# Sharing the experts' weight split between VectorE and GpSimd: 1280 and 768 of 2048 columns

## The reference

```python
def moe_ffn(x, router_w, w1, w2):
    xt = x.reshape(-1, d)
    logits = (xt @ router_w).astype(jnp.float32)
    top_logit, top_idx = lax.top_k(logits, TOP_K)
    gates = jax.nn.softmax(top_logit, axis=-1)
    ...
    def expert_group(args):
        x_blk, e = args
        return swiglu(x_blk, w1[e], w2[e])
    yb = lax.map(expert_group, (xb, blk_expert)).reshape(cap, d)
    ...

for layer in range(DEPTH):
    h = h + parallel_mixer(h, ...)
    h = h + memory_cross_attention(h, mem, ...)
    hn = rms_norm(h, ffn_norm_w[layer])
    if layer % 2 == 0:
        h = h + swiglu(hn, ffn_w1[layer // 2], ffn_w2[layer // 2])
    else:
        h = h + moe_ffn(hn, moe_router[layer // 2], moe_w1[layer // 2], moe_w2[layer // 2])
return rms_norm(h, final_norm_w)
```

## Time and profile before

| | us |
|---|---|
| median of three runs | 1603.72 |
| lowest, highest run | 1603.5, 1607.22 |
| the profiled execution | 1604.92 |
| its span, first to last instruction | 1603.0 |
| PE, DVE, ACT, POOL busy in the span | 1518.2, 1205.3, 910.7, 17.2 |

### The profile page before, as it was taken

One profiled execution on the slowest core, in us unless ns is written; L12 is line 12 of the kernel. 1 busy time (PEld: TensorE's weight loads), 2 busy tenths in 40 slices (PEclk: granted clock), 3 DMA queues, 4 the chain that ended last, 5 costly groups with the idle time before them and its releaser, 6 DMA issues.

```text
span 1603.0 us, 21501 instructions
## 1 busy us (share of the span) xinstructions
PE 1518.2 (95%) x8381; PEld 1316.1 (82%) x8381; DVE 1205.3 (75%) x1154; ACT 910.7 (57%) x865; POOL 17.2 (1%) x17
## 2 busy tenths in 40 slices
PE   6998999899998998999799999999999999999995
PEld 5887988899987887987688888888878888888884
DVE  5787654545445787654499898998988999898995
ACT  5534343444434534343377777777777777777772
POOL 0000100000000000100000000000000000000000
PEclk9997999999999998999699999999999999999997
DMA  7332342355554342351379998999989999899992
GB/s 289 132 133 78 132 161 102 133 184 184 184 202 164 132 136 76 132 179 58 157 275 359 381 352 341 346 362 377 352 317 356 362 367 360 346 353 374 364 359 90
DMA packets 54176, 390.45 MB, mean 244 GB/s; under 512 B 5952, under 2 KB 5952, under 8 KB 7360
## 3 DMA queue, kind: packets, MB, share of 16 engines
q1 hardware_dynamic: 53536, 386.97, 64.4%
q10 hardware_dynamic: 544, 2.10, 0.3%
HBM read 388.00 MB, written 1.05 MB: 243 GB/s over the span
## 4 chain that ended last, share of the span: by engine, by line
issue 52%; PE 38%; DVE 6%; ACT 2%; DMA 1%; POOL 0%; SPq 0%; DVEq 0%; POOLq 0%; ACTq 0%
PE pb L807 11%; PE pb L808 11%; PE pb L809 11%; DVE arena L1352 1%; DVE arena L1481 1%; PE pb L987 1%; DVE wlo L1233 1%; ACT whi L504 1%; PE pb L800 1%; DVE arena L1466 1%; DMA params<-in_par 0%; PE pb L955 0%; DVE arena L1465 0%; PE pb L1009 0%; DMA kvX<-in_ffn_w 0%
## 5 line engine op out<-in xcount | busy, mean ns | idle before, releaser
L1733 DVE TENSOR_TENSOR wlo<-raw,whi 128x2048 fp32r<-128x2048 f32 x175 | 400.5, 2291 | 52.0 <-ACT whi L737 49.9
L737 ACT ACTIVATE whi<-raw 128x2048 fp32r<-128x2048 f32 x175 | 335.8, 1920 | 136.1 <-PE pb L809 136.1
L1233 DVE TENSOR_TENSOR wlo<-raw,whi 128x2048 fp32r<-128x2048 f32 x101 | 230.0, 2287 | 137.0 <-ACT whi L504 136.9
L504 ACT ACTIVATE whi<-raw 128x2048 fp32r<-128x2048 f32 x101 | 193.4, 1917 | 228.0 <-PE pb L809 227.6
L807 PE MATMUL pb<-whi,mTh 128*128 128x512 f32 x768 | 305.7, 398 | 4.7 <-DVE kvXr L1733 3.5
L809 PE MATMUL pb<-whi,mTl 128*128 128x512 f32 x768 | 300.7, 391 | 0.0
L807 PE MATMUL pb<-xTh,whi 128*128 128x256 f32 x736 | 210.7, 286 | 3.4 <-DVE xTl L1270 3.4
L1733 DVE TENSOR_TENSOR kvXr<-kvX,whi 128x2048 fp32r<-128x2048 f32 x86 | 196.6, 2290 | 19.3 <-ACT whi L737 17.7
L808 PE MATMUL pb<-xTl,whi 128*128 128x256 f32 x736 | 208.6, 283 | 0.0
L809 PE MATMUL pb<-xTh,wlo 128*128 128x256 f32 x736 | 208.6, 283 | 0.0
L808 PE MATMUL pb<-wlo,mTh 128*128 128x512 f32 x528 | 205.6, 389 | 0.0
(11 more groups left out here) (286 smaller groups left out, 2154.3 us busy)
## 6 DMA issues: line engine op xcount, KB each, us to landing
raw<-in_ffn_w SPq DMA_DIRECT2D x209, 1024.0 KB, 4.8
kvX<-in_ffn_w SPq DMA_DIRECT2D x88, 1024.0 KB, 4.8
raw<-in_lin_w SPq DMA_DIRECT2D x68, 1024.0 KB, 4.7
arena<-in_mem ACTq DMA_DIRECT2D x2, 1024.0 KB, 8.0
h<-in_x SPq DMA_DIRECT2D x1, 1024.0 KB, 4.8
out<-xn SPq DMA_DIRECT2D x1, 1024.0 KB, 4.0
consts<-in_con SPq DMA_DIRECT2D x1, 906.0 KB, 6.5
params<-in_par SPq DMA_DIRECT2D x1, 654.0 KB, 7.6
```

Source lines behind the costliest of these rows:

```text
L504: nc.scalar.activation(whi[:, m % HRING, :], raw[:, m % RING, :], ACT.Copy).then_inc(hi_ready, 1)
L737: nc.scalar.activation(whi[:, (MOE0 + c) % HRING, :], xraw_slots[c % XRING], ACT.Copy).then_inc(hi_ready, 1)
L1233: V.tensor_tensor(wlo[:, m % RING, :], raw[:, m % RING, :], whi[:, m % HRING, :].bitcast(F32), ALU.subtract).then_inc(lo_ready, 1)
L1733: V.tensor_tensor(xlo_slots[c % XRING], xraw_slots[c % XRING], whi[:, (MOE0 + c) % HRING, :].bitcast(F32), ALU.subtract).then_inc(lo_ready, 1)
```

## The change

`LO_DVE = 1280` is new. In the experts' stage VectorE's subtraction covers columns 0 to 1279 of each chunk, and GpSimd makes the same subtraction for columns 1280 to 2047 (768 columns). GpSimd waits for the same `hi_ready` as VectorE and counts up a semaphore of its own, `lo_pool`. PE waits for both. Since a matmul has room for fewer waits than are wanted now, PE gets another instruction for every chunk of the code. GpSimd has a loop over all four pairs (66 chunks each), and reads `over_flag` behind it, ahead of the final norm. The dense layer and the projections are as before.

```diff
--- before.py
+++ after.py
@@ -47,6 +47,7 @@
 XRING = 6
 HRING = 3
 PASSES = 2
+LO_DVE = 1280
 LIN = 17
 LIN_CHUNKS = 2 * LIN
 W1_CHUNKS = NF
@@ -301,6 +302,7 @@
         slot_loaded = [sem(f"slot_loaded{i}") for i in range(RING)]
         hi_ready = sem("hi_ready")
         lo_ready = sem("lo_ready")
+        lo_pool = sem("lo_pool")
         w_used = sem("w_used")
         x_in = sem("x_in")
         mem_in = sem("mem_in")
@@ -486,6 +488,22 @@
                 root(slice(8, 10))
                 root_rows()
                 root_rows()
+
+            def split_experts(p):
+
+                with pool.Fori(0, NE // 2) as pair:
+                    for c in range(2 * FFN_CHUNKS):
+
+                        pool.wait_ge(hi_ready, pair * (2 * FFN_CHUNKS) + (moe_chunk(p) + c + 1))
+                        nc.gpsimd.tensor_tensor(xlo_slots[c % XRING][:, LO_DVE:], xraw_slots[c % XRING][:, LO_DVE:],
+                                                whi[:, (MOE0 + c) % HRING, LO_DVE:].bitcast(F32),
+                                                ALU.subtract).then_inc(lo_pool, 1)
+
+            split_experts(0)
+            pool.wait_ge(routed_ok, 1)
+            more = pool.value_load(over_flag[0:1, :].bitcast(U32), min_val=0, max_val=1)
+            with pool.If(more):
+                split_experts(1)
             root_rows()
 
 
@@ -1139,6 +1157,7 @@
                         def ready(c):
 
                             pe.wait_ge(lo_ready, expert * FFN_CHUNKS + (MOE0 + c + 1))
+                            pe.wait_ge(lo_pool, expert * FFN_CHUNKS + (c + 1))
                             n = MOE0 + e * FFN_CHUNKS + c
                             return whi[:, n % HRING, :], xlo_slots[(n - MOE0) % XRING]
 
@@ -1279,8 +1298,8 @@
             def first_chunk(p, c):
 
                 dve.wait_ge(hi_ready, moe_chunk(p) + c + 1)
-                V.tensor_tensor(xlo_slots[c], xraw_slots[c], whi[:, (MOE0 + c) % HRING, :].bitcast(F32),
-                                ALU.subtract).then_inc(lo_ready, 1)
+                V.tensor_tensor(xlo_slots[c][:, 0:LO_DVE], xraw_slots[c][:, 0:LO_DVE],
+                                whi[:, (MOE0 + c) % HRING, 0:LO_DVE].bitcast(F32), ALU.subtract).then_inc(lo_ready, 1)
 
             def add_rows(name, layer, half):
 
@@ -1730,7 +1749,8 @@
                             while done[0] <= m and not (last and e * FFN_CHUNKS + done[0] >= 2 * FFN_CHUNKS):
                                 c = e * FFN_CHUNKS + done[0]
                                 dve.wait_ge(hi_ready, pair * (2 * FFN_CHUNKS) + (moe_chunk(p) + c + 1))
-                                V.tensor_tensor(xlo_slots[c % XRING], xraw_slots[c % XRING], whi[:, (MOE0 + c) % HRING, :].bitcast(F32),
+                                V.tensor_tensor(xlo_slots[c % XRING][:, 0:LO_DVE], xraw_slots[c % XRING][:, 0:LO_DVE],
+                                                whi[:, (MOE0 + c) % HRING, 0:LO_DVE].bitcast(F32),
                                                 ALU.subtract).then_inc(lo_ready, 1)
                                 done[0] += 1
```

## The result

| | before | after |
|---|---|---|
| median, us | 1605.12 (four runs, the three of before and one more) | 1664.39 (four runs, 1662.96 to 1664.92) |
| span of the profiled execution, us | 1603.0 | 1662.3 |
| experts' loops, VectorE's first subtraction to the end of its last, us | 765.3 | 822.3 |

The changed kernel is slower, by a ratio of 1.0364 (95% interval 1.0349 to 1.0379), that is 59 us; 57 us of them lie in the experts' loops. In the two profiles another 2.9 us lie ahead of the last norm before the experts, where both kernels do the same work (its scaling starts at 777.03 and at 779.91 us); that is scatter between executions.

A forecast was written before the change was run, and what follows sets the result against it. PE was taken to bound the kernel. In series, 261 chunks x 3.20 us gave 835 in place of 765 us, +70, and jumps +3: 1678 us profiled, 1677 us as median; range 1600 to 1735 us.

The forecast's parts named there:

- PE bounds the stage, the freed time of VectorE is worth nothing: Experts' stage: PE busy 760.6 of 765.3 us, so VectorE's 0.80 us a chunk, 209 us in all, helps nobody.
- rival A: Experts' subtractions on VectorE and GpSimd exclude each other, read from a 16-column power: 1645 to 1730 us expected, chance 0.70.
- B: Experts' subtractions on both engines run side by side, nothing late: 1602 us, chance 0.13.
- C: Experts' subtractions share access in turn, both get longer: 1604 to 1635 us, chance 0.09.
- D: PE's stops at the loop's jump back wait for the low half and go away: 1597 us, chance 0.03.
- E: GpSimd over 2.1 us in series, or PE's clock falling often under exclusion: over 1735 us, chance 0.05.
- VectorE's part, 1.49 us: Experts' loops: VectorE's subtraction, cut from 2048 to 1280 columns, takes 1.49 us.
- GpSimd's part, 1.71 us: Experts' loops: GpSimd's 768 columns at twice VectorE's time a column plus 0.10 us, range 1.4 to 2.1 us.
- The sum a chunk, 3.20 us: Experts' loops: both subtractions one after the other, 1.49 + 1.71 us, over the stage's mean of 2.93 us a chunk.
- "Lose nothing there": Stretches where PE does matmuls that aren't chunk work: the subtractions run on, so nothing given back or lost.
- The jumps back, 3 us: GpSimd's three jumps to its loop's start cost half of 3 x 1.8 us, +3 us; 0 if slack hides them.
- PE's further instruction, 0: PE's added instruction a chunk is hidden while it waits for GpSimd: 0, up to 8 us if exposed.

The follow-up runs named there:

- first and second experiment: Changed kernel with GpSimd's subtraction made a write-only memset: 1607.53 us, ratio 1.0007; changed kernel with VectorE's 1280-column instruction reading one input: 1606.25 us, ratio 0.9999.
- the strict order: Changed kernel with GpSimd waiting for VectorE's half of the same chunk before its own: 1724.43 us, ratio 1.0748.
- an experiment: Changed kernel with VectorE's additions of the experts' outputs cut from 512 to 32 columns each: 1654.55 us, ratio 1.0325.
- the last experiment: Changed kernel with GpSimd's first subtraction held back until the first pair's tokens are selected: 1659.65 us, ratio 1.0330.
- the kernel with 1024 columns: Changed kernel with the split moved from 1280 columns on VectorE to 1024 on each engine: 1736.10 us, ratio 1.0814.

## Why the prediction was right, point by point

- **PE bounds the stage, the freed time of VectorE is worth nothing.** Right. Where nothing excludes (first and second experiment) VectorE was 0.80 us a chunk quicker and the ratio was 1.0007 and 0.9999.
- **The two halves exclude each other** (rival A, 0.70). Right, and from the row that it was read from. Rivals B, C and D are out: in the strict order GpSimd keeps its 1.84 us while VectorE's instruction stands still beside it. E is out too, with GpSimd at 1.855 us and a granted clock of 1.00 over the loops. The Trainium skill's rule (SBUF — State Buffer, "Who interferes with whom") holds here as far as it was put in the forecast: two inputs on VectorE against a GpSimd instruction that reads exclude each other (3.06 us for the two), and a write-only memset beside the two-input subtraction costs nothing (1493 ns).
- **VectorE's part, 1.49 us.** Right: 1493 ns.
- **GpSimd's part, 1.71 us.** Too small by 0.145 us: 1.855 alone. Twice VectorE's rate was right: the shortest lengths for 256, 512, 768 and 1024 columns are 0.73, 1.26, 1.80 and 2.34 us, which is 2.10 ns a column and 0.19 us. Too small was the fixed part, which I had taken at 0.10 us from a memset, and in the loops the subtraction takes 0.05 us more than its shortest. (The expectation for 1024 columns has 2.2 ns, from a length in the loops at 768 and a shortest length at 256.)
- **The sum a chunk, 3.20 us.** Mis-sized: 3.06. This is the term that was off. I added whole lengths, but 0.14 us of each, 0.28 us together, lie under the other's run. With GpSimd's length too small by 0.145 us, 261 x 0.14 = 37 us too much are left.
- **"Lose nothing there" for the stretches between chunks.** This step failed, in the other direction. 261 x 3.06 is 799 us, and the loops took 822: 23 us were lost. 9 to 10 us are the additions: 1.39 us a time, which I hadn't set against GpSimd's 1.8 us; I had only set the 0.8 us of the rounds. The other 13 us lie in the second experts of the first three pairs, which are 3 to 6 us over 33 beats each. What makes them up is only a reading. The selection of the next pair is held up there by 0.9 us (1.20 for 0.28). And at a pair's end, where PE gathers, GpSimd stands idle for 2.77 and 2.08 us until ScalarE has a high half, which waits for PE:

```profile
992.25 1.85 POOL L498 TENSOR_TENSOR kvXr<-kvX,whi 128x768 fp32r<-128x768 f32 x1 [2.77 <-ACT whi L755]
1005.35 1.84 POOL L498 TENSOR_TENSOR wlo<-raw,whi 128x768 fp32r<-128x768 f32 x1 [2.08 <-ACT whi L755]
```

- **The jumps back, 3 us.** Not seen apart from the above. Behind the first one GpSimd stands idle for 4.46 us, but what it waits for is again ScalarE and so PE, which had stopped for 2.5 us itself at its own jump (1.64 us before).
- **PE's further instruction, 0.** Within what can be told, right.
- **PE's clock, 0.** Right for the loops: the mean granted clock was 1.00 there, before and after. Ahead of them it wasn't the same, see below.
- **The sum in the loops.** Forecast 70 + 3 us, measured 57. The account is 70 - 37 + 23 = 56 us; of the 23, which is a remainder, an experiment shows 10. So the time came out within 13 us of the forecast in part by luck: two errors of opposite sign. And the range of 1600 to 1735 us also held rivals B and C, so that the time alone told little; what told were the lengths and the beat.
- **Nothing ahead of the loops.** This I had overlooked: GpSimd's first three subtractions aren't in the loops' time. They begin as soon as its last norm is done, beside the scaling of that very norm, and took 3.07 + 1.33 us of VectorE's path. From the scaling to the selection both profiles take 20.3 us all the same, since PE worked there at a higher clock after. The stretch of the router's matmuls, before and after:

```profile
781.00:792.30 11.30, 11.21 (x54) 11.12 (x52) 3.40 (x12) 2.08 (x6) 0.00 (x0) 0.50 0.01 1
```

```profile
786.50:795.10 8.60, 8.57 (x56) 8.48 (x54) 3.81 (x11) 2.48 (x6) 0.00 (x0) 0.70 0.01 2
```

  The granted clock was 0.50 before, which is 1.2 GHz throughout, and 0.70 after, partly 2.4 GHz, for the same work in 11.3 and 8.6 us. In the profile of the last experiment it was 0.50 again. Why it was granted more after the longer scaling no run shows. The hold-up's price is told apart by the kernel with 1024 columns, at 0.50 like the kernel before.
- **What I said would show it.** The lengths, the beat and ScalarE's idle time did. Three signs did not, as a profile doesn't show them: the records of the two subtractions overlap, since a length includes the standing still; PE's waits for them are few; and PE is shown busy for 97% of the stage and not for about 90%, for the reason given with the result.

## What to carry to other kernels

Before work is moved from VectorE to GpSimd, ask what both read at that moment. If VectorE's instruction has two inputs in SBUF and GpSimd's reads SBUF, the two run in series, so the test is whether their lengths together, less some 0.25 us, stay under the beat of the engine that bounds the stage; and here GpSimd takes twice as long per column, so every column moved makes the sum longer. Look too at what else VectorE does when GpSimd's first instruction can start. And if the moved work was hidden already, as it was here, even a clean split gains nothing.

## What the runs showed of the hardware that was not expected

- In series, the pair takes 0.24 to 0.28 us less than its two lengths alone (3.06 against 1.49 + 1.855; 2.77 against 1.75 + 1.26), some 0.14 us for each; 3.33 when a semaphore forces the order.
- A length in the profile includes the time that an instruction stands still for the other engine: VectorE's 1024-column subtraction, 1.21 us at its shortest, is shown with 2.68 us in the median.
- One-input instructions of VectorE can be held up by GpSimd too: the product with a scalar at 1024 columns in 0.75 us, by GpSimd's subtraction (1.42 to 4.49 us a pair) and by its memset (to 2.53 us). A sum over an axis of length 1, at 1.16 ns a column, isn't held up by the subtraction. Whether speed or kind decides isn't shown.
- From the end of VectorE's subtraction to the start of the one of GpSimd that waits for its semaphore it was 0.14 us, in a beat of 3.33 us.
